# Spreading the product steps of the attention stages anew over their units

## The reference, cut to what matters

```python
for l in range(DEPTH):                       # DEPTH = 2
    ...
    o_na = neighbourhood_attend(na_q, na_k, na_v, cna_k, cna_v, na_rpb[l])    # 8 heads of 64, with a bias
    o_mla = softmax_attend(m_q, m_k_all, m_v_all)                             # 8 heads of 96
    o_diff = diff_attend(d_q, d_k_all, d_v_all, lam)                          # 4 heads, two maps each
    y = (sigmoid(g_na) * ((o_na * silu(z_na)) @ w_br[0])
         + sigmoid(g_mla) * ((o_mla * silu(z_mla)) @ w_br[1])
         + sigmoid(g_diff) * ((o_diff * silu(z_diff)) @ w_br[2]))
    x_new = x + gate * (y @ w_out)
```

## Time and profile before

| what | value |
|---|---|
| median of 3 runs (lowest, highest) | 2517.69 us (2517.47, 2520.54) |
| the profiled execution's own time | 2518.32 us |
| its span, first to last instruction | 2516.2 us |
| PE busy | 2388.2 us (95%) |
| DVE, ACT, POOL busy | 1575.4 (63%), 1212.7 (48%), 447.2 us (18%) |
| near: layer 0, layer 1 | 1447.8 to about 1556.7, 2128.8 to about 2204.7 us |
| mla: layer 0, layer 1 | 1594.2 to about 1713.6, 2236.1 to about 2304.8 us |
| maps: layer 0, layer 1 | 1814.1 to about 1924, 2380.3 to about 2453 us |

### The profile page before, as it was taken

One profiled execution on the slowest core, in us unless ns is written; L12 is line 12 of the kernel. 1 busy time (PEld: TensorE's weight loads), 2 busy tenths in 40 slices (PEclk: granted clock), 3 DMA queues, 4 the chain that ended last, 5 costly groups with the idle time before them and its releaser, 6 DMA issues. The chain is left out here.

```text
span 2516.2 us, 35199 instructions
## 1 busy us (share of the span) xinstructions
PE 2388.2 (95%) x13732; PEld 1959.0 (78%) x13732; DVE 1575.4 (63%) x2368; ACT 1212.7 (48%) x2080; POOL 447.2 (18%) x276
## 2 busy tenths in 40 slices
PE   7998899999999999998999999999999989989989
PEld 5776777887878888788998767677777878778779
DVE  5878778778645666787675454643565355464675
ACT  2646535323328334556454355663365243566364
POOL 0000000000016444000003431004211135403310
PEclk9999999999999999999999999999999989999999
DMA  8654435666425332446663231213222233334335
GB/s 316 212 159 148 143 87 164 200 175 191 121 76 151 91 86 68 134 126 165 185 180 100 74 93 53 60 51 89 67 75 65 79 92 106 104 82 118 84 85 151
DMA packets 416076, 302.13 MB, mean 120 GB/s; under 512 B 10210, under 2 KB 389192, under 8 KB 414888
## 3 DMA queue, kind: packets, MB, share of 16 engines
q1 hardware_dynamic: 414800, 299.45, 41.1%
q10 hardware_dynamic: 1112, 0.44, 0.1%
HBM read 298.80 MB, written 1.05 MB: 119 GB/s over the span
## 5 line engine op out<-in xcount | busy, mean ns | idle before, releaser
L221 ACT ACTIVATE weights_hi<-wslots 128x1024 fp32r<-128x1024 f32 (+1 forms) x408 | 427.3, 1051 | 264.1 <-PE psum L284 200.8
L284 PE MATMUL psum<-input_hi,weights_hi 128*128 128x512 f32 (+1 forms) x1424 | 511.7, 359 | 3.6 <-PEq L1030 1.8
L284 PE MATMUL psum<-input_hi,weights_lo 128*128 128x512 f32 (+1 forms) x1424 | 498.8, 350 | 0.0
L284 PE MATMUL psum<-input_lo,weights_hi 128*128 128x512 f32 (+1 forms) x1424 | 498.1, 350 | 0.0
L231 POOL TENSOR_TENSOR weights_lo<-wslots,weights_hi 128x1024 fp32r<-128x1024 f32 (+1 forms) x139 | 332.6, 2400 | 733.1 <-ACT weights_hi L221 732.4
L231 DVE TENSOR_TENSOR weights_lo<-wslots,weights_hi 128x1024 fp32r<-128x1024 f32 x269 | 331.2, 1239 | 163.6 <-ACT weights_hi L221 163.0
L284 PEld LDWEIGHTS psum<-input_hi,weights_hi 128*128 128x128 f32 x1424 | 269.6, 189 | 49.6 <-issue 10.8
L284 PEld LDWEIGHTS psum<-input_lo,weights_hi 128*128 128x128 f32 x1424 | 268.9, 189 | 39.8 <-issue 3.1
L284 PEld LDWEIGHTS psum<-input_hi,weights_lo 128*128 128x128 f32 x1424 | 269.0, 189 | 38.7
L284 PE MATMUL psum<-ffn_hidden_hi,weights_hi 128*128 128x512 f32 (+1 forms) x512 | 173.5, 339 | 0.0
L284 PE MATMUL psum<-ffn_hidden_hi,weights_lo 128*128 128x512 f32 (+1 forms) x512 | 172.1, 336 | 0.0
(11 more groups left out here) (521 smaller groups left out, 4886.5 us busy)
## 6 DMA issues: line engine op xcount, KB each, us to landing
wslots<-w_in SPq DMA_DIRECT2D x132, 512.0 KB, 3.9
wslots<-ffn_w SPq DMA_DIRECT2D x128, 512.0 KB, 4.6
wslots<-ssd_w_in SPq DMA_DIRECT2D x49, 512.0 KB, 4.0
h<-w_ada SPq DMA_DIRECT2D x32, 512.0 KB, 4.3
wslots<-ada_w SPq DMA_DIRECT2D x32, 512.0 KB, 4.7
wslots<-gla_w_in SPq DMA_DIRECT2D x25, 512.0 KB, 5.0
input_raw<-ada_w SPq DMA_DIRECT2D x24, 512.0 KB, 4.0
ada_slab<-ada_w SPq DMA_DIRECT2D x24, 512.0 KB, 3.9
```

Source lines behind the costliest of these rows:

```text
L221: act.activation(self.part(self.whi_r, n), self.slot(n), ACT.Copy)\
L284: ins = pe.matmul(out_of(self.bank(g)), l, r, start=first and i == 0, stop=last and i == len(pairs) - 1, skip_group_check=not (first and l ...
```

## The change

`fill_marks` is rewritten and the PE order at the head of each stage is changed. Nothing is computed differently and no instruction is added or removed; only the places of the steps (and with them, of the finishing work of the tiles, of roundings, splits and loads) move.

- Before, mark n was `S * n + S + S // 2`. After, the first mark is `lead + 2 * S // 3` with `lead = S + S // 2`, and the rest of the steps is spread evenly, up to the total at the last unit.
- In mla and maps the stage still begins with `S // 2` steps, but then come `scores(0)`, steps up to `lead` = S + S // 2, `scores(1)`, `turn(0)` and steps up to the first mark. Before, `scores(1)` followed `scores(0)` directly, half of S stood between `scores(1)` and `turn(0)`, and half of S behind `turn(0)`.
- In near, `scores(0)`, steps up to `lead` (the old first mark, so unchanged), `scores(1)`, `turn(0)`, and now steps behind `turn(0)`, where there were none.

| stage | marks before | marks after |
|---|---|---|
| near, layer 0 | 7, 12, 17, 22, ... 77, 80 | 10, 14, 19, 24, 28, 33, 38, 42, ... 75, 80 |
| mla and maps, layer 0 | 9, 15, 21, 27, ... 93, 96 | 13, 18, 24, 29, 35, 40, 46, 51, ... 90, 96 |
| near, layer 1 | 15, 25, 35, ... 75, 80 | 21, 29, 37, 46, 54, 63, 71, 80 |
| mla and maps, layer 1 | 18, 30, 42, ... 90, 96 | 26, 36, 46, 56, 66, 76, 86, 96 |

```diff
--- before.py
+++ after.py
@@ -3211,11 +3211,10 @@
                 b.split_weights(dve, "dve", k0 + 3)
 
 
-def fill_marks(N, S):
-
-
-    marks = [S * n + S + S // 2 for n in range(N)]
-    return [min(x, S * N) for x in marks[:-1]] + [S * N]
+def fill_marks(N, steps, first):
+
+
+    return [first + (steps - first) * n // (N - 1) for n in range(N)]
 
 
 def attend_pairs(b, l, r, m, last, fill):
@@ -3230,7 +3229,9 @@
     N = len(units)
     NEAR = 2 * PAIRS if near else 0
     S = fill.steps // N
-    marks = fill_marks(N, S)
+    early = 0 if near else S // 2
+    lead = S + S // 2
+    marks = fill_marks(N, fill.steps, lead + 2 * S // 3)
     OUT, SCORE, TURNED = 0, (4, 5), (6, 7)
     st = ExitStack()
     with st:
@@ -3341,28 +3342,26 @@
                     for _ in range(a, e):
                         next(products)
 
-                lead = marks[0] if near else S // 2
                 if near:
                     pe.wait_ge(b.sem("normed"), b.nth("normed", 0))
                     pe.wait_ge(b.sem("deviation_ready"), b.nth("deviation_ready", 0))
                     scores(0)
-                    steps(0, lead)
+                    steps(early, lead)
                     pe.wait_ge(*b.evacuated(sum(b.phases[f"na_z{l}"][2:]) - 1))
                 else:
                     pe.wait_ge(b.sem("unit_scaled"), b.nth("unit_scaled", 0))
                     pe.wait_ge(b.sem("values_copied"), b.nth("values_copied", 0))
-                    steps(0, lead)
+                    steps(0, early)
                     pe.wait_ge(b.sem("tile_copied"), b.nth("tile_copied", 0))
                     scores(0)
+                    steps(early, lead)
                 for n in range(N):
                     if n + 1 < N:
                         scores(n + 1)
-                    if n == 0:
-                        steps(lead, max(S, lead))
                     turn(n)
                     if n:
                         values(n - 1)
-                    steps(start(n) if n else max(S, lead), marks[n])
+                    steps(start(n) if n else lead, marks[n])
                 values(N - 1)
                 for _ in products:
                     pass
@@ -3709,7 +3708,8 @@
     units = [(gq, h) for gq in range(len(groups)) for h in range(DFH)]
     N = len(units)
     S = fill.steps // N
-    marks = fill_marks(N, S)
+    early, lead = S // 2, S + S // 2
+    marks = fill_marks(N, fill.steps, lead + 2 * S // 3)
     SCORE, TURNED, OUT, FLIPPED = (4, 5), 6, 7, 0
     def keys(n):
         return T if groups[units[n][0]][0] == LAT else NCTX
@@ -3787,22 +3787,20 @@
                     for _ in range(a, e):
                         next(products)
 
-                lead = S // 2
-                steps(0, lead)
+                steps(0, early)
                 pe.wait_ge(b.sem("lam_exps"), b.nth("lam_exps", 0))
                 scores(0)
+                steps(early, lead)
                 for n in range(N):
                     gq, h = units[n]
                     if n + 1 < N:
                         scores(n + 1)
-                    if n == 0:
-                        steps(lead, S)
                     turn(n)
                     if n:
                         values(n - 1)
                     if gq and h == 2:
                         turn_rows(gq - 1)
-                    steps(start(n) if n else S, middle(n))
+                    steps(start(n) if n else lead, middle(n))
                 values(N - 1)
                 for _ in products:
                     pass
```

## The result

| kernel | median us (lowest to highest, runs) | ratio to before, 95% interval |
|---|---|---|
| before | 2519.55 (2515.86 to 2525.76, 14) | |
| after | 2527.45 (2522.99 to 2530.35, 14) | 1.0031 (1.0024 to 1.0039) |

The change makes the kernel slower by 0.31%, 7.9 us, where 2513.6 was forecast with a range that ended at 2521.

A forecast was written before the change was run, and what follows sets the result against it. PE, busy 95% of the span, bounds the kernel, so only its idle or low-clock time can be gained. Terms -3.8 - 1.7 - 0.4 - 2.7 + 3.0 + 1.5 = -4.1 took the median 2517.69 to 2513.6 us, range 2505 to 2521.

The forecast's parts named there:

- mla of layer 0: Steps fill the head gap, nothing new is waited for, gap and clock loss go: -3.8 us (bounds -4.5 and -2.3).
- near, layer 0: Three steps fill the gap, but the chain of bias loads and POOL's masking ends where it did: -0.4 us (-3 to +2).
- near, layer 1: A 4.7 us gap ahead of scores(2), later bank waits at tiles 1 and 6 gone: -2.7 us (-5 to +1).
- the 2.0 us that were read off one execution against 2151.24: In near of layer 1, 24 steps are done 2.0 us earlier than before, where PE waited 2.07 for tile 1's bank.
- maps, layer 0: Head gain partly lost to waits for DVE and neighbouring sigmoid tiles, some regained at the end: -1.7 us (-3.5 to +1).
- turn(3) and turn(4) each wait some 0.6 us more: 1.0 is left: In maps of layer 0, tile 1's sigmoid directly after tile 0's cuts the 2.1 us lead at turn(2) to 1.0.
- At the end one step more stands behind the last values, worth 0.7: In maps of layer 0, one extra step fills time where PE waits at the end, gaining 0.7 us.
- mla, layer 1: Head waits of 1.7 us for slot 2 and 3.4 for tile 0's bank, then more table loads: +3.0 us (+0.5 to +6).
- the 1.9 that the chain of ACT and DVE was to cost: In mla of layer 1, ACT and DVE take longer per unit than PE, losing another 1.9 us by scores(7).
- maps, layer 1: Head waits of 2.1 and 3.2 us, ACT and DVE then set the pace, 0.9 back at the end: +1.5 us (-0.5 to +4.5).
- Slower: Rival: low-clock stretches behind layer 1's gaps (4.5 us more) and table loads (up to 10 more) give 2524 us; chance 0.13.
- Layer 0 gains nothing that lasts: Rival: maps and near of layer 0 and near of layer 1 give back all, 2516 to 2519 us; chance 0.15.

The follow-up runs named there:

- head_only: Kernel after with the old marks, keeping only the new order at the head of mla and maps; 2522.97 us, ratio 1.0011 to before.
- before_copy: Kernel before with the gates' sigmoid replaced by a plain copy in both maps stages; 2517.16 us in one run.
- c_mla1: Kernel before with the new order and marks in near and mla of both layers, maps left old; 2514.52 us, ratio 0.9986 to before.
- maps_finish: Kernel after, but in maps of layer 0 the engines other than PE follow the earlier of old and new mark; 2523.05 us in one run.
- after_copy: Kernel after with the gates' sigmoid replaced by a plain copy in both maps stages; 2507.01 us in one run.
- marks_only: Kernel before with only the new marks, keeping the old order at the head; 2524.79 us, ratio 1.0019 to before.
- c_maps0_copy: Kernel before with new order and marks in layer 0 and near of layer 1, sigmoid a copy in maps of layer 0; 2504.79 us, ratio 0.9948 to before.
- decoupled: Kernel after with PE's order kept, but the other engines following the old marks; 2545.81 us, ratio 1.0103 to before.

## Why the prediction was wrong

**What bounds the kernel, and mla of layer 0:** right. The gap went with its clock loss: -4.6 for -3.8, of which 0.8 is a clock loss ahead of the change's first step that only the profile of before has.

**near, layer 0:** right in kind. PE waits 0.34, 0.79, 0.74 and 0.58 us for exponentials where it waited 2.44; -1.6 for -0.4, within its bounds.

**near, layer 1:** the mechanism came as told, one wait of 4.7 us and none at tile 3:

```profile
2140.22 0.58 PE L3500 MATMUL psum<-input_hi,weights_hi 128*128 128x256 f32 x1 [4.74 <-DVE mla_cq_lo L3549]
```

But the gain of -1.9 is mostly not the change's. head_only and before_copy leave this stage as it was and have -1.7. The profile of before had the clock at 0.72 in two stretches of 6 us, the second behind the 2.07 gap of the earlier trace rows; that of before_copy has one, and 1.00 around its second gap of 0.95 (before, then before_copy):

```profile
2150.00:2156.00 6.00, 4.75 (x17) 2.61 (x19) 3.00 (x7) 3.20 (x7) 3.73 (x4) 0.72 0.32 101
```

```profile
2144.00:2150.00 6.00, 5.84 (x24) 3.80 (x26) 2.52 (x6) 3.35 (x9) 1.85 (x3) 0.50 0.52 137
2154.00:2160.00 6.00, 5.05 (x39) 3.38 (x38) 3.45 (x7) 3.32 (x7) 3.04 (x3) 1.00 0.34 108
```

The step that failed is the 2.0 us that were read off one execution against 2151.24; against a profile without that second loss the change gives about 0.2.

**maps, layer 0: the step that turned the sign.** "turn(3) and turn(4) each wait some 0.6 us more: 1.0 is left" was right in its two delays: turn(3) came 0.6 later and turn(4) another 0.6. But only five steps stand between these turns now instead of six, which the sum left out (0.7), so 0.2 was left and not 1.0. And it stopped there: the working never listed the tiles of units 5 to 15. The pairing of sigmoid tiles comes back in units 4 and 5 and in 13 and 14, and in units 5 and 13 the sigmoid meets the square root and its table. By the turns that cost 1.2 us at turn(7) and 1.5 at turn(15), with 0.6 between them that are not the tables'. "At the end one step more stands behind the last values, worth 0.7" failed too: PE arrived at the last turn too early and idled 1.27, and the wait behind the last values is 2.84 instead of 2.46 all the same. Predicted -1.7, measured +4.9: 3.7 at the end of the stage, and 1.2 of clock in the untouched work behind it. The runs without the sigmoid show that the exchanges turned the sign.

**mla, layer 1:** +3.0 predicted, +4.1 measured (+5.5 and +6.2 elsewhere), by three errors. The clock loss behind the second gap, 1.7 us, was left out, although the text had put 1.5 on any gap over 2 us, and that gap was 0.8 longer than told (4.2 for 3.4). And the 1.9 that the chain of ACT and DVE was to cost did not come: the exponentials do come 7.27 and 8.56 us apart (2265.57, 2272.84, 2281.40), but turns follow at PE's own 7.24 and 7.35 without a wait, probably since PE left the head late and ACT and DVE had caught up meanwhile. These three leave 0.5 of the 4.1 without an account.

**maps, layer 1:** +1.5 predicted, +5.1 measured. The two waits were right in place and size. Scores(3) were put at 2403.9 and came at 2406.96, 3.1 later (3.4 with the 0.35 by which this profile entered the stage early). Most of it is the two clock losses of the head, again left out: 0.95 in the scores behind the first gap and 1.6 in the six steps behind the second, and some in the turn and the steps between. The chain of ACT and DVE was then to cost 2.5 up to scores(7) and cost 1.1: these came at 2435.25. Its term has an error of its own: scores(7) were put at 2433.6 instead of 2431.17, but with 76 steps done against 78, so 0.7 more should have been counted. The 0.9 that the end was to give back did not come: the last turn waits 2.47 instead of 1.78.

**The rivals.** "Slower" had its mechanism half right: stretches at 1.2 GHz behind the gaps of layer 1, in two stages and not in near. It held no word on maps of layer 0, and its 2524 is 6 us above the kernel before, where 7.9 were measured, so its near hit is in part luck. "Layer 0 gains nothing that lasts" came nearest for layer 0 (-1.3 in all). The Trainium skill, "ScalarE: Activation LUTs", section "What ACT_TABLE_LOAD costs", has 2.66 us for a change of tables; here the load is 1.28 and the sigmoid starts 1.30 behind its start (1828.03, 1829.33), and the chain of 7.34 us has no room for more. The price of one exchange was read rightly; what was missed is where the exchanges fall.

Open is what decides whether the clock falls behind a gap of 1.8 us: it did in c_mla1 and maps_finish and not in after and after_copy. Open is also why marks_only costs so little in mla of layer 1 and so much in maps.

## What to carry to other kernels

When marks are moved, write down for every unit, up to the last, which tiles it finishes and what else the other engines do in it; here eight sigmoids in every second unit cost nothing that could be seen, and the same eight, three times in neighbouring units, twice beside a square root with its own table and with PE's late units shortened, cost 5.3 us of waits, and 8 to 11 with what followed behind the stage. Filling a gap at the head pays only where slots and banks for those steps are free at that time, and where the engines behind have slack to keep what PE gains; try such a change stage by stage, since a sum of gains and losses hides the stage that pays. A price read from one execution should be looked up in a second one before a term rests on it.

## What the runs showed of the hardware that had not been expected

- An idle gap of about 2 us is followed by scores at the lower clock in some executions and not in others of the same code: 1.88 and 3.28 us for the same product behind the same gap of 1.76 us. A stage with such gaps scatters by 1 to 2 us; mla of layer 0 without them came out at -4.6 eight times in nine.
- The same 12 matmuls behind the wait for `diff_rows` at the end of maps of layer 0 took 2.79 us where that wait was 1.4 (after_copy, c_maps0_copy) and 3.9 to 5.1 where it was 2.1 to 2.9. But decoupled has 4.0 behind 1.5, so the length of the wait alone doesn't settle it.
- The part ahead of the first stage, the same in all kernels, ended between 3.8 us earlier and 2.9 us later than in the profile of before. That is as much as the whole effect that was asked for.
